# First tile of a gated linear recurrence layer: units 0 and 1 side by side on half weights, three warm-up products, squares summed for one product

## The reference, cut to what matters

```python
h = _rmsnorm(x, norm_g)                        # x * rsqrt(mean(x^2) + eps) * norm_g
z = h @ w_in                                   # 2080 x 1024 by 1024 x 5120
fgate = lb + (1.0 - lb) * jax.nn.sigmoid(f)    # lb: a softmax of lb_logits
logf = jnp.log(fgate); kin = 1.0 - fgate
qf = jax.nn.silu(q) * (DK ** -0.5)
S = decay * S + k outer v; o = scores @ v + q @ S     # per head, in chunks of 32 tokens
```

## Time and profile before

| | |
|---|---|
| median of 3 runs | 1374.6 us (1374.36 to 1375.0) |
| span of the profiled execution, first to last instruction | 1372.1 us |
| what the median has beyond that span | 2.5 us |
| TensorE busy | 1359.5 us, 99% |
| VectorE, ScalarE, GpSimd busy | 932.0, 685.6, 198.4 us |
| mean granted TensorE clock | 0.998 |
| first product of unit 0 | at 7.81 us |

### The profile page before, as it was taken

The page is one execution under the profiler, slowest core; times in us unless marked ns, Lnnn a source line. Parts: engine busy times, 40 slices in busy tenths (PEclk is TensorE's granted clock), DMA queues, the critical chain, the costliest instruction groups (busy, mean ns, idle before and its releaser), DMA issues.

```text
span 1372.1 us, 21266 instructions
## 1 busy us (share of the span) xinstructions
PE 1359.5 (99%) x8272; PEld 1345.2 (98%) x8272; DVE 932.0 (68%) x1642; ACT 685.6 (50%) x992; POOL 198.4 (14%) x200
## 2 busy tenths in 40 slices
PE   9999999999999999999999999999999999999997
PEld 7999999999999999999999999999999999999997
DVE  7899655668975456788844567987445689964443
ACT  6565444355664344556643445665433556653332
POOL 2003021110031211001212110012220200130001
PEclk9999999999999999999999999999999999999999
DMA  6544533246535333465363335653532476534338
GB/s 207 140 131 127 208 122 122 94 130 200 143 108 212 118 123 107 129 193 147 98 222 110 121 110 144 171 156 126 189 122 96 136 170 205 178 108 173 118 100 94
DMA packets 140259, 195.91 MB, mean 143 GB/s; under 512 B 83712, under 2 KB 100480, under 8 KB 138496
## 3 DMA queue, kind: packets, MB, share of 16 engines
q1 hardware_dynamic: 140160, 194.56, 47.1%
HBM read 174.91 MB, written 19.61 MB: 142 GB/s over the span
## 4 chain that ended last, share of the span: by engine, by line
PE 92%; DVE 5%; DMA 1%; issue 1%; ACT 1%; SPq 0%; DVEq 0%; ACTq 0%
PE Z L519 29%; PE Z L521 28%; PE Z L520 28%; DVE wlo L1038 1%; DMA wraw<-w_all 1%; PE B L575 1%; PE B L668 1%; PE B L658 1%; PE B L552 0%; DVE xres L1441 0%; DVE snew L1198 0%; DVE h_b L1078 0%; PE B L519 0%; PE B L521 0%; PE B L520 0%
## 5 line engine op out<-in xcount | busy, mean ns | idle before, releaser
L1038 DVE TENSOR_TENSOR wlo<-wraw,whi 128x1024 fp32r<-128x1024 f32 x280 | 367.0, 1311 | 299.7 <-ACT whi L796 299.5
L519 PE MATMUL Z<-hhi,whi 128*128 128x416 f32 x1576 | 552.7, 351 | 0.0
L520 PE MATMUL Z<-hlo,whi 128*128 128x416 f32 x1576 | 549.4, 349 | 0.0
L521 PE MATMUL Z<-hhi,wlo 128*128 128x416 f32 x1576 | 549.4, 349 | 0.0
L796 ACT ACTIVATE whi<-wraw 128x1024 fp32r<-128x1024 f32 x280 | 295.9, 1057 | 425.2 <-PE Z L521 353.0
L519 PEld LDWEIGHTS Z<-hhi,whi 128*128 128x128 f32 x1576 | 296.0, 188 | 0.9 <-issue 0.6
L520 PEld LDWEIGHTS Z<-hlo,whi 128*128 128x128 f32 x1576 | 296.0, 188 | 0.5
L521 PEld LDWEIGHTS Z<-hhi,wlo 128*128 128x128 f32 x1576 | 295.9, 188 | 0.3
L521 PE MATMUL Z<-mhi,wlo 128*128 128x416 f32 x320 | 112.3, 351 | 0.0
L520 PE MATMUL Z<-mlo,whi 128*128 128x416 f32 x320 | 111.9, 350 | 0.0
L519 PE MATMUL Z<-mhi,whi 128*128 128x416 f32 x320 | 111.5, 348 | 0.0
(11 more groups left out here) (252 smaller groups left out, 1555.2 us busy)
## 6 DMA issues: line engine op xcount, KB each, us to landing
wraw<-w_all SPq DMA_DIRECT2D x280, 512.0 KB, 3.5
xres<-xT SPq DMA_DIRECT2D x5, 1664.0 KB, 7.5
xin<-xT SPq DMA_DIRECT2D x4, 1664.0 KB, 7.8
yT<-xres SPq DMA_DIRECT2D x4, 1664.0 KB, 8.9
v_blocks<-h_vt SPq DMA_DIRECT2D x80, 52.0 KB, 3.1
vtm<-v_blocks SPq DMA_DIRECT2D x20, 192.0 KB, 3.9
ktm<-k_blocks SPq DMA_DIRECT2D x20, 192.0 KB, 3.6
k_blocks<-kt SPq DMA_DIRECT2D x64, 52.0 KB, 1.9
```

What stands on the lines that cost most here:

```text
L519: pe.matmul(out, wh, xh, start=first, stop=False)
L520: pe.matmul(out, wh, xl, start=False, stop=False)
L521: return pe.matmul(out, wl, xh, start=False, stop=final)
L1038: dve.tensor_tensor(wlo[n % RING][:], raw(t, n)[:], whi[n % RING][:].bitcast(F32), ALU.subtract).then_inc(wlo_made, 1)
```

## The change

Five edits, all for the first tile:

1. SP loads weights 0 and 1 in two halves of 512 columns each (blocks 0 to 3 LEFT, 4 to 7 RIGHT), both left halves behind the first pair of inputs; `cst` is issued by ScalarE.
2. ScalarE and VectorE split these halves one by one (`split_half`), between the high and low parts of the inputs; the square of block 0 comes behind the two left halves.
3. TensorE runs units 0 and 1 side by side (`first_pair`) in place of `first_unit` and `late_low(1)`: pair of blocks by pair of blocks, into Z0 and Z1. WARM is 3.
4. VectorE makes the six additions of squares ahead of the split of weights 2, and one more of the two sums; `x_squares` is one product, after the fourth block of unit 2 (which the title calls unit 3, counting from one).
5. VectorE splits weights 5 in slot 2 of the tile, after the scaling of q, and no longer in the preamble.

```diff
-WARM = 4
+WARM = 3
@@ SP
-                if i == 0:
-                    sp.dma_start(cst[:], consts).then_inc(cst_landed, 16)
-                if i == 0:
-                    sp.dma_start(wraw[0][:], w_all[0]).then_inc(w_landed[0], 16)
-            sp.dma_start(wraw[1][:], w_all[1]).then_inc(w_landed[1], 16)
+                if i == 0:
+                    for n in range(2):
+                        sp.dma_start(wraw[n][:, LEFT], w_all[n, :, LEFT]).then_inc(w_half_landed[n], 16)
+                elif i < 3:
+                    sp.dma_start(wraw[i - 1][:, RIGHT], w_all[i - 1, :, RIGHT]).then_inc(w_landed[i - 1], 16)
@@ TensorE
+            def first_pair():
+
+                def high(u, k):
+                    pe.wait_ge(whi_half_made if k < KD // 2 else whi_made, u + 1)
                     pe.wait_ge(hhi_made, k + 1)
+                    pe.matmul(Z[u][:, 0:T], whi[u][:, k * P:(k + 1) * P], hhi[k][:], start=(k == 0), stop=False)
...
+                for k in range(0, KD, 2):
+                    if k == 2:
+                        for i in (k, k + 1):
+                            for u in range(2):
+                                high(u, i)
+                                low_weights(u, i)
+                            for u in range(2):
+                                low_input(u, i)
+                        continue
+                    for u in range(2):
+                        for i in (k, k + 1):
+                            high(u, i)
+                            low_input(u, i)
+                        for i in (k, k + 1):
+                            mm = low_weights(u, i)
+                        if k == KD - 2:
+                            mm.then_inc(acc_done, 1)
...
-                    if u == 2 and k == 3:
+                    if k == 4:
                         x_squares()
...
-                for i in range(2):
-                    pe.wait_ge(x0_summed, KD - 3 + i)
-                    mm = pe.matmul(B4[:, 0:T], ones_r[:].bitcast(F32), h0[i][:], start=(i == 0), stop=(i == 1))
-                mm.then_inc(xssq_done, 1)
+                pe.wait_ge(x0_summed, KD - 1)
+                pe.matmul(B4[:, 0:T], ones_r[:].bitcast(F32), h0[0][:], start=True, stop=True).then_inc(xssq_done, 1)
@@ ScalarE
+            act.dma_start(cst[:], consts).then_inc(cst_landed, 16)
             act.preload_act_table_set(LN_EXP)
...
+            def split_half(n, c, landed, made):
+                act.wait_ge(landed[n], 16)
+                act.activation(whi[n][:, c], wraw[n][:, c], ACT.Copy).then_inc(made, 1)
...
             weighted_hi(0)
             weighted_hi(1)
+            split_half(0, LEFT, w_half_landed, whi_half_made)
+            split_half(1, LEFT, w_half_landed, whi_half_made)
             square(0)
-            split(0, 0)
             weighted_hi(2)
             weighted_hi(3)
-            for k in range(4, KD):
-                weighted_hi(k)
-            split(0, 1)
+            split_half(0, RIGHT, w_landed, whi_made)
+            weighted_hi(4)
+            weighted_hi(5)
+            split_half(1, RIGHT, w_landed, whi_made)
+            weighted_hi(6)
+            weighted_hi(7)
             square(1)
             split(0, 2)
@@ VectorE, in tile(), slot s
                     if first(t) and s:
                         scale(*UNITS[s - 1])
+                    if first(t) and s == 2:
+                        split(0, 5)
@@ VectorE, preamble
-            split(0, 1)
-            split(0, 2)
             for k in range(2, KD):
                 dve.wait_ge(xsq_made, k + 1)
...
                 dve.tensor_tensor(h0[k % 2][:], h0[k % 2][:], h0[k][:], ALU.add).then_inc(x0_summed, 1)
+            dve.wait_ge(x0_summed, KD - 2)
+            dve.tensor_tensor(h0[0][:], h0[0][:], h0[1][:], ALU.add).then_inc(x0_summed, 1)
+            split(0, 2)
             split(0, 3)
             bounds()
             split(0, 4)
-            split(0, 5)
```

More of the change, by code:

```diff
@@ L294, in step_kernel @@
         lbe_made = sem("lbe_made")
+        w_half_landed = [sem(f"w_half_landed{i}") for i in range(2)]
+        whi_half_made, wlo_half_made = sem("whi_half_made"), sem("wlo_half_made")
+        LEFT, RIGHT = slice(0, D // 2), slice(D // 2, D)
         wlo_made, kin_made, b_made, d_made = sem("wlo_made"), sem("kin_made"), sem("b_made"), sem("d_made")
@@ L706, in tile @@
                         if s == 0:
-                            first_unit()
-                        else:
+                            first_pair()
+                        elif s == 2:
                             late_low(s)
@@ L739, in tile, with low_input, low_weights @@
                     y_squares(t, True)
[L741 to L746, removed]
+            def first_pair():
+                def high(u, k):
+                    pe.wait_ge(whi_half_made if k < KD // 2 else whi_made, u + 1)
                     pe.wait_ge(hhi_made, k + 1)
-                    pe.matmul(out, whi[0][:, c], hhi[k][:], start=(k == 0), stop=False)
+                    pe.matmul(Z[u][:, 0:T], whi[u][:, k * P:(k + 1) * P], hhi[k][:], start=(k == 0), stop=False)
+                def low_input(u, k):
                     pe.wait_ge(hlo_made, k + 1)
[L750 to L753, removed]
+                    pe.matmul(Z[u][:, 0:T], whi[u][:, k * P:(k + 1) * P], hlo[k][:], start=False, stop=False)
+                def low_weights(u, k):
+                    pe.wait_ge(wlo_half_made if k < KD // 2 else wlo_made, u + 1)
+                    return pe.matmul(Z[u][:, 0:T], wlo[u][:, k * P:(k + 1) * P], hhi[k][:], start=False,
+                                     stop=(k == KD - 1))
+                for k in range(0, KD, 2):
[15 more added lines that the diff above has]
+                            mm.then_inc(acc_done, 1)
             def late_low(u):
@@ L1499, in counts, with split_half @@
                 dve.reciprocal(rc[:], rc[:]).then_inc(rc_used, 1)
+            def split_half(n, c, hi_made, made):
+                dve.wait_ge(hi_made, n + 1)
+                dve.tensor_tensor(wlo[n][:, c], wraw[n][:, c], whi[n][:, c].bitcast(F32), ALU.subtract).then_inc(made, 1)
             weighted_lo(0)
             weighted_lo(1)
-            split(0, 0)
+            split_half(0, LEFT, whi_half_made, wlo_half_made)
+            split_half(1, LEFT, whi_half_made, wlo_half_made)
             weighted_lo(2)
             weighted_lo(3)
-            for k in range(4, KD):
-                weighted_lo(k)
-            split(0, 1)
-            split(0, 2)
+            split_half(0, RIGHT, whi_made, wlo_made)
+            weighted_lo(4)
+            weighted_lo(5)
+            split_half(1, RIGHT, whi_made, wlo_made)
+            weighted_lo(6)
+            weighted_lo(7)
             for k in range(2, KD):
```

## The result

The changed kernel takes 1378.15 us (median of 8 runs, 1377.24 to 1380.68), the kernel before in the same job 1374.36 (1373.85 to 1375.0): 3.8 us slower, ratio 1.003 [1.0021, 1.0038]. Its profiled execution took 1377.84 us with a span of 1375.7. The forecast had slower, by 1.7; the time lies 0.25 us over the range.

What follows compares the result with a forecast made beforehand. TensorE, busy 99% of the span, was taken as the bound, but waiting on VectorE near 52 us. Its lead is spent and the chain 1.7 us late: span 1372.1 + 1.7 = 1373.8, plus 2.5 gives 1376.3 us; range 1373.2 to 1377.9.

Steps and rivals of the forecast that it cites:

- TensorE's chain: First tile's start: first product 1.27 us sooner, low clock giving back 0.4; lead of 1.3 us after unit 2.
- the wait for the squares: In unit 2 TensorE reaches the summed squares near 17.5 us and waits 1.0 us for the last addition.
- The lead at the scores: TensorE's head start from the first units, 1.3 us after unit 2, carried to the scores of unit 8.
- VectorE's chain: First scaling unchanged near 22.65 us; later split 5 delays weights 7, so head 0's cumulative sum comes 1.7 us late.
- The load of weights 7: Issued at 27.33 us after split 5, it takes 3.6 us and is there at 31.0.
- Rivals A: The lead survives to the end of the kernel: 1.3 us kept, 1373.3 us; chance 0.10.
- B: Weights 7 hold nobody up and only VectorE's direct 0.45 us delay stays: 1375.05 us; chance 0.11.
- D: The half-loads land late, so the early start of unit 0 fails; end the same unless inputs are late; no chance given.
- The last part of the keys ... lands 3.6 us later: Head 0's keys, landing at 46.2 us before, take 3.6 us from issue again and land at 47.9.
- TensorE waits some 2.4 us: After the scores of unit 8, near 45.5 us, TensorE waits 2.4 us for the keys.
- Rival C: The clock falls to its low level in the wait before the keys: 1.6 us more, 1377.9 us; chance 0.13.
- The end: After L668 all engines shift alike, 1.7 us reach the end (span 1373.8), and the median stands 2.5 us over the span.

Runs made afterwards that it cites:

- a1: Changed kernel with split 5 one slot earlier (slot 1, behind the scaling of f): 1375.59 us, kernel before 1374.23.
- f2: e1 without the 60 waits, so the changed kernel with split 5 in slot 1 and the sigmoid's table loaded ahead: 1374.49 us, kernel before 1374.33.
- d1: Changed kernel with 60 waits added at the start of TensorE's program: 1376.8 us, kernel before 1374.42.
- d2: Changed kernel with split 5 in slot 1, the sigmoid's table loaded ahead and the 60 waits: 1373.47 us, kernel before 1374.42.
- c2: Kernel before with 12 small unread products ahead of unit 3 of tile 0: 1374.38 us, kernel before 1374.02.
- d3: a1 with the 60 waits at the start of TensorE's program, no table loaded ahead: 1373.69 us, kernel before 1374.42.
- e1: The kernel of d2 measured again in another job: 1373.24 us, kernel before 1374.04.
- e3: d1 with 14 unread filler products in TensorE's wait for the keys: 1375.6 us, kernel before 1374.04.
- a3: Changed kernel with weights 6 and 7 of tile 0 loaded into the start's buffers, free sooner: 1376.12 us, kernel before 1374.23.
- f1: e1 with two warm-up products in place of three: 1373.76 us, kernel before 1374.33.

## Why the prediction was right or wrong

**TensorE's chain: right in its terms, two of them mis-sized.** First product at 6.53 (6.54 forecast). The low clock lasted until 8.4, not 7.8, and cost 0.8, not 0.4; the wait for the squares was 0.2 us and not 1.0, since the inputs landed sooner and everything of the start's chain stood 0.45 us earlier. The lead at the scores is 1.7 us against 1.3; it would be further off if the two had not partly cancelled.

**VectorE's chain: right in its order, and its sum partly by luck.** Split 5 at 25.62 (26.1 less the 0.45), weights 7 issued at 26.87, ScalarE's split at 31.24 (31.0), cumulative sum at 34.78 (34.56): 1.89 us late, 1.7 forecast. The load of weights 7 was mis-sized: 4.3 us, not 3.6, and the early start of 0.45, which I had not forecast either, hid most of it. Rivals A and B fell here, and D by the first product at 6.53.

**"The last part of the keys ... lands 3.6 us later": the step that failed.** It carried a duration from the kernel before to a place in time where something else ran: 5.4 us, 1.8 more. The instruction queue stood on the page and I read past it, and I took the duration from one issue, where the same trace has keys of 5.2 and 5.4 us at 311 and 912 us.

**"TensorE waits some 2.4 us", and so the clock stays: failed by it.** The wait was 5.0 us: the keys landed 2.0 later than forecast, and TensorE asked 0.5 sooner. Rival C's mechanism came in on top, at a price of 1.5 to 1.8 us (1.6 written). I gave it 0.13, because the wait stood just under the 2.6 us read at the end of the trace; a1 lost its clock around a wait of 2.3, f2 around one of 2.2. So 2.6 was no bound, and my own 2.4 was not on its safe side.

**The end: nearly right.** From head 1 to the last tile both kernels run alike within 0.2 us, then 0.6 of the loss comes back, where I had "1.7 us reach the end"; the median stands 2.45 us over the span, as assumed.

In all the late chain was sized within 0.2. The missing 2.1 us are about the keys' 1.8 and the clock's 1.5 to 1.8, less the 0.8 of waits at L658 and L668 that the forecast had added and the later keys covered, and less the 0.6 that came back towards the end.

## What to carry to other kernels

When an edit moves a chain that ends in a transfer, don't carry the transfer's duration along: look at what its DMA engines do at the new time, TensorE's own instruction packets among it. A wait of two or three microseconds on TensorE is to be priced twice, once as it stands and once with the clock's fall. And put a moved step where its engine idles: one slot earlier, split 5 gave back 2.6 of the 3.8 us. With the table ahead and the packet out of the way of the keys (the 60 waits) the pairing came out 0.8 and 0.95 us below the kernel before, each time with an interval that holds 1; without the 60 waits it was no faster (f2, 1374.49 against 1374.33).

## What the runs showed of the hardware

- TensorE's instructions come in packets of 16 KB; those near the first keys took 0.9 to 1.5 us each. By the times of the packets they run on the DMA engines that also move the data: keys of which a part stood behind one landed some 1.5 to 2 us late (seven traces against thirteen). The Trainium skill (Runtime: NRT & Kernel Launch, "Instruction fetch mechanics") says that an engine's sequencer fetches 16 KiB blocks of 256 instructions by a DMA queue of its own, and calls the cost "mostly hidden". The size agrees (1.08 MB over 66 packets). Between 30 and 75 us no wait of TensorE's loads belongs to such a packet; its data did wait, and in the changed kernel the keys came 1.8 us later by it and what ran around it.
- Beside such a packet SP's issue of a transfer often took longer: 1.25 us in d1 (packet at 40.7), 1.50 in d2 (41.2), 1.51 in c2 (41.8), 1.93 in d3 (41.5), 1.74 in e1 (40.5), 1.21 in e3 (40.9), where the same instruction otherwise takes 0.37 to 0.49. Not always: the issue at 46.52 in the changed kernel, beside the packet of 46.59, took 0.34. In all twenty traces 171 of 804 issues beside a packet took over 0.9 us, and 199 of the 10251 others; why, no run shows. From d1's chain and from e1's timeline of SP's queue:

```profile
40.92 1.25 SPq L484
```

```profile
40.51 1.74 SPq L504 DMA_DIRECT2D vtm<-v_blocks  x1
```

- By their times, the clock fell in some executions of one kernel and not in others (a1, a3, d1, f2), which gives a3 two groups of times 1.8 us apart. It fell 2.0 us after the end of the last product in f2, 2.5 in a1, 3.5 in d1 and 4.4 in the changed kernel, and stayed up through an idle stretch of 2.9 us in a3 and 2.4 in f1. In a1 the products had started again 0.3 us before the fall.
- 60 waits, for a value that was there long before the last of them, put TensorE's first warm-up product 1.6 us later.
